# First gated embedding: input products ahead of the second gate, x of the first column half added and flipped while the second gate is multiplied

## The chip, the cores and the metric

The kernel runs on one core of a Trainium2 chip. The time is that of the device, in microseconds, for one execution of the whole program. Work is done by TensorE (matrix products), VectorE and ScalarE (elementwise), GpSimd (a little) and SyncE, which issues the loads.

## What is computed

Fourteen stages on an activation x of 256 rows by 1024 columns, in float32. The change is in the tenth, the first "gated embedding", and in what surrounds it. From the reference, cut to that stage and its neighbours:

```python
x = x + 0.5 * swiglu(rms_norm(x, ln_ffn2[i]), ffn2_w_gu[i], ffn2_w_down[i])    # stage g2.0
gate = jax.nn.sigmoid(rms_norm(x, ln_ple[i]) @ ple_w_gate[i])                  # stage pl0 (i = 0)
x = x + gate * (p[i] @ ple_w_in[i])
x = x + 0.5 * swiglu(rms_norm(x, ln_ffn1[i]), ffn1_w_gu[i], ffn1_w_down[i])    # stage g1.1 (next i)
```

The gate's weight is 1024 by 1024, `p[i]` is 256 by 256 and `ple_w_in[i]` 256 by 1024.

## The kernel before

**Split products.** A product of float32 matrices is made of three passes: each operand is split into a rounded high part and a low part (the difference), and high by high, high by low and low by high are added in PSUM (`mm3`). For a weight, ScalarE copies the high part from `ring` to `WH` (`hi`) and VectorE subtracts to give the low part in `WL` (`lo`), in parts of 1024 columns; two pieces of weights fit in `WH` and `WL`. For x, TensorE transposes it ("flip", L208) into PSUM, ScalarE scales the result by the norm's gain into the high part `XH` (`flip_act`) and VectorE forms the low part `XL` (`flip_dve`); both lie in the tile `XBt`. A flip is done in two halves: half 0 is columns 0 to 511 of x (eight blocks of 128 become kt 0 to 3), half 1 the rest (kt 4 to 7). Within a half, `i` is one of two groups of 128 rows. The norm's row factor is applied later, so products can start before the sum of squares is known; the squares are ScalarE's (`square`).

**The gated embedding `pl0`** (`ple`). The gate is computed in two column halves n = 0 and 1, each from two pieces of weights, `pl_g0_0.0`, `pl_g0_0.1` and `pl_g1_0.0`, `pl_g1_0.1`. `tms_pe` multiplies one gate: for each piece c (kt 4c to 4c+3) and each i, 12 matmuls of 512 columns. So a gate is 48 matmuls. `p @ w_in` ("input products") is not split: 8 float32 matmuls of 512 columns, read straight from `ring` and recorded as 16 passes. ScalarE takes a tanh of each gate result (two per gate), VectorE does two operations per half and i: `T2 = (tanh + 1) * product`, then `x = 0.5 * T2 + x`. The semaphore value named `pl0.x{i}{n}` says that x of rows i, columns n is there. The transposes of the next stage's flip (`follow[t].pe`) wait on it.

**The next stage `g1.1`** (`ffn`) has 22 pieces `g1.1.0` to `g1.1.21` of 3072 columns: parts 0 and 1 are gate and up weights, part 2 the output weights. Pieces 0 and 1 need 48 matmuls of 256 columns each, from piece 2 on a product takes 32 matmuls; after the product of piece j (from 2 on) follow 12 matmuls with the output weights of piece j-2 (they read `HHt` and `HLt`).

**Queues.** Each engine has one list of instructions, in the order in which the stage functions are called; no engine overtakes within its list. `ring` has three slots of 3072 columns, taken in turn. SyncE's list of loads is fixed: a piece's first part is loaded when parts 0 and 1 of the piece that held the slot have been split, its last 1024 columns (`rear`) when part 2 has been. `pl_p_0` and `pl_i_0`, the operands of the input products, take a slot each; the loads of `g1.1.1` and `g1.1.2` wait for the last input product, whose semaphore value has the name `pl_i_0`. PSUM's eight banks are given out in the order in which TensorE's list asks for them.

Of the kernel before, what the change touches and what calls it, by code (L numbers as in the profile page):

```python
# [248 lines left out]
def build(nc, wts, vecs, rows4, rowb, cons, rgw, xin, out):  # L249
    ctx = ExitStack()  # L250
    with ctx:
# [29 lines left out]
        X = v3(Xt[:, :], 2)  # L281
# [237 lines left out]

        n_ss, n_x, n_r, n_h, n_t, n_q, n_s4, n_s5, n_f = sm(2), sm(2), sm(2), sm(2), sm(2), sm(2), sm(4), sm(4), sm(2)  # L520
        DG, RB = work[:, NW - 512:NW - 256], work[:, NW - 256:NW]
        follow = {}

        def flip_pe(P, t, src, half, key):

# [28 lines left out]
        def flip_pool(G, t):  # L554

            for q in range(4):
                sl = slice(2 * q, 2 * q + 2)
                G.wait_ge(f"{t}.xl{q}")
                G.tt(XF[:, sl, :], XH[:, sl, :].bitcast(F32), XL[:, sl, :].bitcast(F32), ADD, inc=f"{t}.xf" if q == 3 else None,
                     back=2 if q else 1)  # L560

        def unscaled(t, g, prev, rows, whole=False):


            SQ4 = work[:, 2048:4096].rearrange("p (n i d) -> p n i d", n=2, i=2)

            def pe(P, half):
                flip_pe(P, t, X, half, lambda i, half: f"{prev}.x{i}{half}")

            def act(A, between=None, early=None):  # L570
                def square(half, i):
                    A.wait_ge(f"{prev}.x{i}{half}")
                    A.act(SQ4[:, half, i, :], X[:, i, half * 512:half * 512 + 512], ACT.Square,
                          accum_out=n_s4[:, 2 * half + i:2 * half + i + 1], inc=(f"{t}.sq" if half else f"{t}.sqa") if i else None)

                flip_act(A, t, g, 0)
                if early:
                    early(A)
                square(0, 0)
                square(0, 1)  # L580
                if between:
                    between(A)
                square(1, 0)
                flip_act(A, t, g, 1)
                square(1, 1)

            def dve(V, q):
                if q < 4:
                    flip_dve(V, t, g, q)
                if q in (4, 5):  # L590
                    V.wait_ge(f"{t}.sq")
                    V.tt(n_ss, n_s4[:, 0:2], n_s4[:, 2:4], ADD)
                    V.ts(n_x, n_ss, 1.0 / 1024, EPS, MUL, ADD)
                    V.rsqrt0(n_r, n_x)
                if q in (4, 6):
                    for k in range(3):
                        V.rsqrt1(n_r, n_x, n_t, inc=f"{t}.nr" if k == 2 else None)
                    for i in range(2) if rows else ():
                        V.ts(DG[:, hs(i)], IDN, n_r[:, i:i + 1], None, MUL, None, inc=f"{t}.dg" if i else None, back=1 + i)

            follow[prev] = Stage(pe, act, dve, (lambda G: flip_pool(G, t)) if whole else None)
            return follow[prev]

# [120 lines left out]
        def ffn(t, g, prev):  # L724
# [113 lines left out]
            def act(A):  # L838
                if first:
                    wh, _, w = start_cut()  # L840
                    A.wait_ge(f"{t}.0:lda")
                    A.act(wh[:, :, 0:256], w[:, :, 0:256], ACT.Copy, inc=f"{t}.0:hia")
                    norm.act(A, early=start_act)
                else:
                    hi(A, f"{t}.0", (0, 1))
                    norm.act(A)
                hi(A, f"{t}.1", (0, 1))
                for j in range(NFF):
                    nx2, b = ahead(f"{t}.{j}"), j % 2
                    if j >= NARROW:  # L850
                        A.wait_ge(f"{t}.{j}:g")
                        A.act(LW[:, b, 0:256], ps[f"{t}.g{j}"][:, 256:512], ACT.Copy, inc=f"{t}.gl{j}")
                    hi(A, nx2, (0,) if j else (0, 1))
                    A.wait_ge(f"{t}.gm{j}")
                    A.act(SG[:, b, :], GU[:, b, 0:256], ACT.Silu, inc=f"{t}.sg{j}")
                    if j < NFF - 1:
                        hi(A, f"{t}.{j}", (2,))
                    if j >= NARROW:
                        A.wait_ge(f"{t}.{j}:u")
                        A.act(LW[:, b, 256:512], ps[f"{t}.u{j}"][:, 256:512], ACT.Copy, inc=f"{t}.ul{j}")  # L860
                    if j < NFF - 1:
                        hi(A, nx2, (1,))
                    if j < NFF - 1:
                        A.wait_ge(f"{t}.h{j}")
                        if j >= 2:
                            A.wait_ge(f"{t}.{j - 2}:d")
                        A.act(HH[:, b, :], H[:, b, :], ACT.Copy, inc=f"{t}.hh{j}")
                    else:
                        split_last_act(A, 0)
                        for i in range(2):  # L870
                            A.wait_ge(f"{t}.h{j}{i}")
                            A.act(HH[:, 2, hs(i)], H[:, b, hs(i)], ACT.Copy, inc=f"{t}.hh{j}{i}")
                        split_last_act(A, 1)
                        hi(A, nx2, (1,))
                    if first:
                        params_act(A, j)
                    if t == "g1.0" and j in (6, 7):
                        A.wait_ge(f"{t}.nf")
                        A.act(X[:, j - 6, :], X[:, j - 6, :], ACT.Copy, scale=n_f[:, j - 6:j - 5], inc=f"{t}.xf{j}")

            def dve(V):
# [5 lines left out]
                        start_dve(V, u)  # L887
                else:
                    lo(V, f"{t}.0", (0, 1))
                for q in range(2 if first else 1, 4):  # L890
                    norm.dve(V, q)
                if t == "g1.0":
                    norm.dve(V, 4)
# [2216 lines left out]
        def ple(t, li, prev):  # L3110
# [3 lines left out]
            T2 = buf(512)  # L3114
            gate = lambda n: (f"pl_g{n}_{li}.0", f"pl_g{n}_{li}.1")

            def pe(P):
                for n in range(2):
                    tms_pe(P, gate(n), 4, 512, t, head=None if n else norm)
                if li:  # L3120
                    return
                wp, wi = v3(raw("pl_p_0"), 2), v3(raw("pl_i_0"), 2)
                for n in range(2):
                    for i in range(2):
                        if n and i and t in follow:
                            follow[t].pe(P, 0)
                        use = f"{t}.pi{n}{i}"
                        ps.take(use)
                        P.wait_ge("pl_p_0:ld", "pl_i_0:ld", *ps.free(use))
                        for kt in range(2):  # L3130
                            last = n == 1 and i == 1 and kt == 1
                            P.mm(ps[use], wp[:, kt, hs(i)], wi[:, kt, n * 512:n * 512 + 512], kt == 0, kt == 1,
                                 inc=("pl_i_0" if last else use) if kt else None)
                        ps.give(use, f"{t}.pie{n}{i}")

            def act(A):
                norm.act(A)
                for n in range(2):
                    hi(A, ahead(gate(n)[0]))
                    if n == 0:  # L3140
                        hi(A, ahead(gate(n)[1]))
                    for i in range(2):
                        last = gate(n)[1]
                        A.wait_ge(last if i else f"{last}:i0", f"{t}.nh")
                        A.act(TH[:, n, i, :], ps[f"{last}/{i}"], ACT.Tanh, scale=n_h[:, i:i + 1], inc=f"{last}.e{i}")

            def dve(V):
                for q in range(1, 5):
                    norm.dve(V, q)
                    if q == 1:  # L3150
                        lo(V, gate(0)[1], (0,))
                V.ts(n_h, n_r, 0.5, None, MUL, None, inc=f"{t}.nh")
                for n in range(2):
                    lo(V, ahead(gate(n)[0]))
                    if n == 0:
                        lo(V, ahead(gate(n)[1]))
                for n in range(2):
                    for i in range(2):
                        xv = X[:, i, n * 512:n * 512 + 512]
                        V.wait_ge(f"{t}.pie{n}{i}" if li else "pl_i_0" if n and i else f"{t}.pi{n}{i}", f"{gate(n)[1]}.e{i}")  # L3160
                        if li:
                            V.stt(T2, TH[:, n, i, :], 1.0, PI[:, n, i, :], ADD, MUL)
                        else:
                            V.stt(T2, TH[:, n, i, :], 1.0, ps[f"{t}.pi{n}{i}"], ADD, MUL, inc=f"{t}.pie{n}{i}")
                        V.stt(xv, T2, 0.5, xv, MUL, ADD, inc=f"{t}.x{i}{n}")
                    if n == 0 and t in follow:
                        follow[t].dve(V, 0)

            def pool(G):
                lo(G, ahead(gate(0)[0]))  # L3170
# [302 lines left out]
```

## Time and profile before

| what | value |
|---|---|
| three runs | 2108.29, 2112.36, 2113.53 us; median 2112.36 |
| the profiled execution | 2112.04 us, of which its span is 2110.2 us |
| granted TensorE clock, mean | 0.997 |
| TensorE busy | 2084.3 us, 99% |
| weight loads busy | 1790.8 us, 85% |
| VectorE busy | 1541.8 us, 73% |
| ScalarE busy | 1289.6 us, 61% |

The span runs from the first instruction to the last; the time has some 1.8 us more. All stretches named below are microseconds from the span's start. Stage `pl0` and the start of `g1.1` lie between 1575 and 1615 us. A TensorE instruction counts as busy from its start to a modelled end, and neighbours overlap, so the distance between starts says more than the duration.

### The profile page before, as it was taken

The numbers are of one execution on the slowest core, as the hardware profiler recorded it, in microseconds if no ns is written. First come the engines' busy times: TensorE is split into PE (matmuls) and PEld (weight loads), VectorE is DVE, ScalarE is ACT, GpSimd is POOL, SyncE is SP. The second block draws the span as 40 slices with busy tenths as digits, with TensorE's granted clock in tenths as the row PEclk, the third lists the DMA queues.
The fourth block names the chain that finished last, engine by engine and source line by source line (L and its number), as shares of the span: only waits on it lengthen the run. The fifth ranks groups of instructions, "written<-read, shape, count | busy, mean of one in ns | idle before, by whom it ended". The sixth has DMA issues, their size and how long they took to land.

```text
span 2110.2 us, 33620 instructions
## 1 busy us (share of the span) xinstructions
PE 2084.3 (99%) x12545; PEld 1790.8 (85%) x12545; DVE 1541.8 (73%) x2787; ACT 1289.6 (61%) x2170; POOL 61.5 (3%) x51
## 2 busy tenths in 40 slices
PE   8999999999999999999999999999999999999999
PEld 7888988888888877888888897888887888988887
DVE  6777888677766677766877677587677776868676
ACT  6656766556555367655665677565565555666555
POOL 0001000000000400000000001000000000000000
PEclk9999999999999999999999999999999999999999
DMA  7553445454555532555455351145445544445452
GB/s 271 185 209 127 159 180 189 180 192 167 210 181 166 180 121 111 193 196 190 166 194 197 126 193 61 71 174 206 180 155 196 203 181 155 164 155 187 180 195 94
DMA packets 74827, 360.76 MB, mean 171 GB/s; under 512 B 17000, under 2 KB 18024, under 8 KB 43816
## 3 DMA queue, kind: packets, MB, share of 16 engines
q1 hardware_dynamic: 74240, 358.08, 46.8%
q8 instruction: 98, 1.61, 0.3%
q14 instruction: 65, 0.53, 0.1%
q0 software_dynamic: 128, 0.26, 0.0%
q10 hardware_dynamic: 296, 0.27, 0.0%
HBM read 357.54 MB, written 1.05 MB: 170 GB/s over the span
## 4 chain that ended last, share of the span: by engine, by line
PE 89%; DVE 5%; ACT 4%; issue 1%; DMA 1%; SPq 0%; DVEq 0%; POOL 0%; ACTq 0%; POOLq 0%
PE ps L203 87%; ACT work L193 2%; DVE WL L121 2%; PE ps L208 2%; DVE work L121 1%; ACT WH L193 1%; DMA ring<-wts 1%; ACT XBt L193 1%; DVE XBt L132 1%; DVE work L132 0%; DVE small L121 0%; DVE small L132 0%; DVE Xt L132 0%; DVE work L158 0%; DVE Xt L121 0%
## 5 line engine op out<-in xcount | busy, mean ns | idle before, releaser
L203 PE MATMUL ps<-XBt,WH 128*128 128x512 f32 (+1 forms) x4144 | 1197.3, 355 | 4.4 <-DVE XBt L132 1.9
L121 DVE TENSOR_TENSOR WL<-ring,WH 128x1024 fp32r<-128x1024 f32 (+2 forms) x653 | 791.3, 1212 | 345.3 <-ACT WH L193 297.9
L193 ACT ACTIVATE WH<-ring 128x1024 fp32r<-128x1024 f32 (+1 forms) x667 | 698.8, 1048 | 345.4 <-PE ps L203 260.9
L203 PE MATMUL ps<-XBt,WL 128*128 128x256 f32 x3352 | 886.5, 280 | 0.0
L203 PEld LDWEIGHTS ps<-XBt,WH 128*128 128x128 f32 x4144 | 718.5, 190 | 105.9 <-DVE WL L121 4.5
L203 PEld LDWEIGHTS ps<-XBt,WL 128*128 128x128 f32 x3352 | 635.6, 190 | 26.6
L203 PE MATMUL ps<-WH,HHt 128*128 128x512 f32 x712 | 278.8, 392 | 0.9 <-DVE WL L121 0.7
L203 PE MATMUL ps<-WH,HLt 128*128 128x512 f32 x712 | 277.2, 389 | 0.0
L203 PE MATMUL ps<-WL,HHt 128*128 128x512 f32 x712 | 277.1, 389 | 0.0
L193 ACT ACTIVATE work<-ps 128x256 f32<-128x256 f32 (+4 forms) x444 | 179.3, 408 | 60.4 <-PE ps L203 21.8
L193 ACT ACTIVATE work<-work 128x256 f32<-128x256 f32 (+6 forms) x222 | 98.7, 445 | 171.1 <-DVE work L121 167.9
L121 DVE TENSOR_TENSOR work<-ps,work 128x256 f32<-128x256 f32 (+3 forms) x376 | 166.1, 442 | 42.4 <-ACT work L193 4.1
L203 PE MATMUL ps<-WH,XBt 128*128 128x512 f32 (+3 forms) x528 | 164.6, 382 | 1.8 <-DVE WL L121 1.3
L203 PEld LDWEIGHTS ps<-WH,HLt 128*128 128x128 f32 x712 | 133.7, 188 | 28.7
L203 PEld LDWEIGHTS ps<-WL,HHt 128*128 128x128 f32 x712 | 133.8, 188 | 28.4
L193 ACT ACTIVATE HHt<-work 128x256 fp32r<-128x256 f32 (+1 forms) x185 | 76.0, 411 | 129.1 <-DVE work L121 127.8
L203 PEld LDWEIGHTS ps<-WH,HHt 128*128 128x128 f32 x712 | 133.7, 188 | 23.4 <-DVE HLt L121 1.4
L121 DVE TENSOR_TENSOR work<-work 128x256 f32<-128x256 f32 (+2 forms) x338 | 142.1, 421 | 12.1 <-ACT work L193 0.7
L203 PE MATMUL ps<-work 64*64 64x64 f32 (+16 forms) x1256 | 116.7, 281 | 2.1 <-ACT work L193 1.9
L203 PEld LDWEIGHTS ps<-WH,XBt 128*128 128x128 f32 x528 | 97.4, 188 | 23.1 <-DVE WL L121 2.9
L203 PEld LDWEIGHTS ps<-work 64*64 64x64 f32 (+6 forms) x1256 | 88.6, 158 | 24.2 <-issue 10.4
L203 PE MATMUL ps<-WL,XBt 128*128 128x512 f32 (+3 forms) x264 | 99.0, 375 | 0.0
(137 smaller groups left out, 1076.8 us busy)
## 6 DMA issues: line engine op xcount, KB each, us to landing
ring<-wts SPq DMA_DIRECT2D x240, 1024.0 KB, 5.8
ring<-wts SPq DMA_DIRECT2D x185, 512.0 KB, 3.8
ring<-wts SPq DMA_DIRECT2D x10, 256.0 KB, 5.0
ring<-wts SPq DMA_DIRECT2D x1, 1152.0 KB, 5.0
Xt<-x SPq DMA_DIRECT2D x4, 256.0 KB, 5.7
out<-Xt SPq DMA_DIRECT2D x4, 256.0 KB, 2.0
ring<-wts SPq DMA_DIRECT2D x1, 768.0 KB, 6.5
work<-wts SPq DMA_DIRECT2D x1, 512.0 KB, 4.6
```

The lines of the kernel that those rows point to most:

```text
L121: self.done(self.e and self.e.tensor_tensor(out, a, b, op), inc)
L132: self.done(self.e and self.e.scalar_tensor_tensor(out, a, s, b, op0, op1), inc)
L193: self.done(self.e and self.e.activation(out, a, f, **kw), inc)
L203: inst = self.e and self.e.matmul(out, l, r, start=start, stop=stop)
L208: inst = self.e and self.e.transpose(out, a, ident)
```

## The change

Four things are done in another order; one call site of a function is moved, nothing is computed otherwise.

- TensorE: the input products of n = 0 (4 matmuls) stand between the two gates; those of n = 1 (4 matmuls) and the transposes of x's half 0 for `g1.1` (8) stand in the middle of the second gate, after its first piece.
- VectorE: x of columns n = 0 is added before the weights of `g1.1.0` are split; the low parts of the flip's half 0 are formed before x of n = 1 is added.
- ScalarE: the high parts of the flip's half 0 are made before the second gate's tanh.
- VectorE: part 2 of `g1.1.0` is no longer split there, but in `ffn`'s loop, at j = 0.

The second gated embedding (`li` = 1) keeps its order.

```diff
-            def act(A, between=None, early=None):
+            def act(A, between=None, early=None, flipped=False):
...
-                flip_act(A, t, g, 0)
+                if not flipped:
+                    flip_act(A, t, g, 0)
...
+            flip_ahead[prev] = lambda A: flip_act(A, t, g, 0)
...
-                    norm.act(A)
+                    norm.act(A, flipped=True) if prev == "pl0" else norm.act(A)
...
-                for q in range(2 if first else 1, 4):
+                for q in range(2 if first or prev == "pl0" else 1, 4):
...
+            def inputs_pe(P, n):
+
+                wp, wi = v3(raw("pl_p_0"), 2), v3(raw("pl_i_0"), 2)
+                for i in range(2):
+                    use = f"{t}.pi{n}{i}"
+                    ps.take(use)
+                    P.wait_ge("pl_p_0:ld", "pl_i_0:ld", *ps.free(use))
+                    for kt in range(2):
+                        last = n == 1 and i == 1 and kt == 1
+                        P.mm(ps[use], wp[:, kt, hs(i)], wi[:, kt, n * 512:n * 512 + 512], kt == 0, kt == 1,
+                             inc=("pl_i_0" if last else use) if kt else None)
+                    ps.give(use, f"{t}.pie{n}{i}")
+
+            def between_pe(P, c, i):
+
+                if c == 0 and i:
+                    inputs_pe(P, 1)
+                    follow[t].pe(P, 0)
+
             def pe(P):
-                for n in range(2):
-                    tms_pe(P, gate(n), 4, 512, t, head=None if n else norm)
-                if li:
-                    return
...
+                tms_pe(P, gate(0), 4, 512, t, head=norm)
+                if not li:
+                    inputs_pe(P, 0)
+                tms_pe(P, gate(1), 4, 512, t, between=None if li else between_pe)
 
             def act(A):
...
+                    if n and t in follow:
+                        flip_ahead[t](A)
                     for i in range(2):
                         last = gate(n)[1]
...
+            def added_dve(V, n):
+
+                for i in range(2):
+                    xv = X[:, i, n * 512:n * 512 + 512]
+                    V.wait_ge(f"{t}.pie{n}{i}" if li else "pl_i_0" if n and i else f"{t}.pi{n}{i}", f"{gate(n)[1]}.e{i}")
+                    if li:
+                        V.stt(T2, TH[:, n, i, :], 1.0, PI[:, n, i, :], ADD, MUL)
+                    else:
+                        V.stt(T2, TH[:, n, i, :], 1.0, ps[f"{t}.pi{n}{i}"], ADD, MUL, inc=f"{t}.pie{n}{i}")
+                    V.stt(xv, T2, 0.5, xv, MUL, ADD, inc=f"{t}.x{i}{n}")
...
-                for n in range(2):
-                    lo(V, ahead(gate(n)[0]))
-                    if n == 0:
-                        lo(V, ahead(gate(n)[1]))
...
+                for k in range(2):
+                    lo(V, ahead(gate(0)[k]))
+                added_dve(V, 0)
+                lo(V, ahead(gate(1)[0]), (0, 1))
+                if t in follow:
+                    for q in range(2):
+                        follow[t].dve(V, q)
+                added_dve(V, 1)
```

How the lists of instructions move is seen best on VectorE and ScalarE, the engines for which TensorE waits in this place. VectorE's list at `pl0`'s end, before; `WL<-ring,WH` splits a part of a weight, `work<-work,ps` and `Xt<-work,Xt` are the two operations that add to x, `XBt<-ps,vt,XBt` is one block of the flip's low part, and `small` belongs to the norm:

```order
L126 TENSOR_SCALAR small<-small 128x2
L121 TENSOR_TENSOR WL<-ring,WH 128x1024 x7
L132 SCALAR_TENSOR_TENSOR work<-work,ps 128x512
L132 SCALAR_TENSOR_TENSOR Xt<-work,Xt 128x512
L132 SCALAR_TENSOR_TENSOR work<-work,ps 128x512
L132 SCALAR_TENSOR_TENSOR Xt<-work,Xt 128x512
L132 SCALAR_TENSOR_TENSOR XBt<-ps,vt,XBt 128x256 x2
```

And VectorE's list at the same place now:

```order
L126 TENSOR_SCALAR small<-small 128x2
L121 TENSOR_TENSOR WL<-ring,WH 128x1024 x4
L132 SCALAR_TENSOR_TENSOR work<-work,ps 128x512
L132 SCALAR_TENSOR_TENSOR Xt<-work,Xt 128x512
L132 SCALAR_TENSOR_TENSOR work<-work,ps 128x512
L132 SCALAR_TENSOR_TENSOR Xt<-work,Xt 128x512
L121 TENSOR_TENSOR WL<-ring,WH 128x1024 x2
L132 SCALAR_TENSOR_TENSOR XBt<-ps,vt,XBt 128x256 x4
```

Of the seven splits four are ahead of the first addition (those of the second gate's weights), two (`g1.1.0`, parts 0 and 1) behind it, and the seventh (part 2) has gone to the loop of `g1.1`. The piece of the difference where it turns up again, on VectorE at j = 0 of that loop, between the product `H` of piece 0 (`work<-work,ps`) and its low part `HLt`:

```order
 L121 TENSOR_TENSOR WL<-ring,WH 128x1024
 L121 TENSOR_TENSOR work<-work,ps 128x256
+L121 TENSOR_TENSOR WL<-ring,WH 128x1024
 L121 TENSOR_TENSOR HLt<-work,HHt 128x256
 L121 TENSOR_TENSOR work<-ps,work 128x256
```

The low part `HLt` of piece 0 now stands one split later, and so does what waits for it. ScalarE's list from the copies of `g1.1.0`'s high parts to the squares of `g1.1`'s norm, as the difference shows it (`work<-ps,small` is a tanh, `XBt<-ps,vt` one block of the flip's high part, `work,small<-Xt` a square with its sum):

```order
 L193 ACTIVATE work<-ps,small 128x512 x2
 L193 ACTIVATE WH<-ring 128x1024 x3
+L193 ACTIVATE XBt<-ps,vt 128x256 x4
 L193 ACTIVATE work<-ps,small 128x512 x2
-L193 ACTIVATE XBt<-ps,vt 128x256 x4
 L193 ACTIVATE work,small<-Xt 128x512 x3
 L193 ACTIVATE XBt<-ps,vt 128x256 x4
```

The flip's half 0 has gone ahead of the second gate's tanh; the three squares and the flip's half 1 stay behind it, in the same order.

## Rows read from the trace of the kernel before

**Rows 1.** The profile page: span, and busy time by engine

```profile
span 2110.2 us, 33620 instructions
...
PE 2084.3 (99%) x12545; PEld 1790.8 (85%) x12545; DVE 1541.8 (73%) x2787; ACT 1289.6 (61%) x2170; POOL 61.5 (3%) x51
```

**Rows 2.** Waits of TensorE, 1586 to 1790 us: waiting group, releaser, us, times, longest

```profile
PE ps L208 <- DVE Xt L132: 1.0, 2, 0.9
```

**Rows 3.** Busy time by stage: stretch, us, each engine (instructions), clock, DMA share, GB/s

```profile
1586.81:1597.69 10.88, 10.88 (x49) 9.01 (x48) 3.47 (x3) 4.48 (x5) 0.00 (x0) 1.00 0.65 242
1597.69:1605.61 7.92, 7.73 (x26) 3.69 (x24) 6.03 (x9) 4.03 (x8) 0.00 (x0) 1.00 0.00 0
1605.61:1614.28 8.67, 7.67 (x58) 6.77 (x57) 7.36 (x15) 6.65 (x15) 0.00 (x0) 1.00 0.84 317
```

**Rows 4.** TensorE in order of time: start us, busy us, instruction, [idle before, releaser]

```profile
1597.69 5.31 PE L203 MATMUL ps<-ring 128*128 128x512 f32 x12
...
1603.63 0.66 PE L208 MATMUL ps<-ct,Xt 128*128 128x128 f32 x4 [0.19 <-DVE Xt L132]
...
1607.43 0.66 PE L208 MATMUL ps<-ct,Xt 128*128 128x128 f32 x4
1608.95 0.66 PE L208 MATMUL ps<-ct,Xt 128*128 128x128 f32 x4 [0.86 <-DVE Xt L132]
1609.55 0.50 PE L203 MATMUL ps<-XBt,WH 128*128 128x256 f32 x2
...
1614.28 0.51 PE L203 MATMUL ps<-XBt,WH 128*128 128x256 f32 x2
...
1626.16 0.39 PE L203 MATMUL ps<-WH,HHt 128*128 128x512 f32 x1
```

**Rows 5.** The same: the first matmul of piece 4's product

```profile
1637.20 0.39 PE L203 MATMUL ps<-XBt,WH 128*128 128x512 f32 x1
```

**Rows 6.** ScalarE in order of time

```profile
1588.17 1.41 ACT L193 ACTIVATE work<-ps,small 128x512 f32<-128x512 f32 x2
1595.56 3.37 ACT L193 ACTIVATE WH<-ring 128x1024 fp32r<-128x1024 f32 x3 [5.98 <-DMA ring<-wts]
...
1605.77 0.63 ACT L193 ACTIVATE work<-Xt 128x512 f32<-128x512 f32 x1
...
1607.41 0.63 ACT L193 ACTIVATE work<-Xt 128x512 f32<-128x512 f32 x1
...
1609.43 1.57 ACT L193 ACTIVATE XBt<-ps,vt 128x256 fp32r<-128x256 f32 x4 [1.29 <-PE ps L208]
...
1628.10 1.06 ACT L193 ACTIVATE WH<-ring 128x1024 fp32r<-128x1024 f32 x1
```

**Rows 7.** VectorE in order of time

```profile
1586.80 2.55 DVE L121 TENSOR_TENSOR WL<-ring,WH 128x1024 fp32r<-128x1024 f32 x2 [0.15 <-ACT WH L193]
1596.66 3.88 DVE L121 TENSOR_TENSOR WL<-ring,WH 128x1024 fp32r<-128x1024 f32 x3 [7.31 <-ACT WH L193]
...
1601.37 0.69 DVE L132 SCALAR_TENSOR_TENSOR Xt<-work,Xt 128x512 f32<-128x512 f32 x1
...
1610.30 1.86 DVE L132 SCALAR_TENSOR_TENSOR XBt<-ps,vt,XBt 128x256 fp32r<-128x256 f32 x4 [0.41 <-ACT XBt L193]
...
1613.00 2.55 DVE L121 TENSOR_TENSOR WL<-ring,WH 128x1024 fp32r<-128x1024 f32 x2 [0.17 <-ACT WH L193]
...
1621.58 0.42 DVE L121 TENSOR_TENSOR work<-work,ps 128x256 f32<-128x256 f32 x1
1622.48 0.42 DVE L121 TENSOR_TENSOR HLt<-work,HHt 128x256 fp32r<-128x256 f32 x1 [0.48 <-ACT HHt L193]
```

**Rows 8.** SyncE's loads into `ring` issued in 1600 to 1610: issue, then landing times

```profile
L196 SPq DMA_DIRECT2D ring<-wts x6: 327/461/686, 1606.0 to 1608.7; - x6
...
DMA to landing us min/median/max: 5.2/8.7/12.2
```

**Rows 9.** The same for the two issued in 1626 to 1627

```profile
DMA to landing us min/median/max: 3.8/4.8/5.9
```

More of the change, by code:

```diff
@@ L521, in build @@
         DG, RB = work[:, NW - 512:NW - 256], work[:, NW - 256:NW]
-        follow = {}
+        follow, flip_ahead = {}, {}
         def flip_pe(P, t, src, half, key):
@@ L3115, in ple @@
             gate = lambda n: (f"pl_g{n}_{li}.0", f"pl_g{n}_{li}.1")
-            def pe(P):
-                for n in range(2):
-                    tms_pe(P, gate(n), 4, 512, t, head=None if n else norm)
-                if li:
-                    return
-                wp, wi = v3(raw("pl_p_0"), 2), v3(raw("pl_i_0"), 2)
-                for n in range(2):
[L3124 to L3134, printed above, removed]
+            def inputs_pe(P, n):
[13 more added lines that the diff above has]
+                    follow[t].pe(P, 0)
+            def pe(P):
+                tms_pe(P, gate(0), 4, 512, t, head=norm)
+                if not li:
+                    inputs_pe(P, 0)
+                tms_pe(P, gate(1), 4, 512, t, between=None if li else between_pe)
             def act(A):
@@ L3152, in dve @@
                 V.ts(n_h, n_r, 0.5, None, MUL, None, inc=f"{t}.nh")
-                for n in range(2):
-                    lo(V, ahead(gate(n)[0]))
-                    if n == 0:
-                        lo(V, ahead(gate(n)[1]))
[L3157 to L3167, printed above, removed]
+                for k in range(2):
[6 more added lines that the diff above has]
+                added_dve(V, 1)
             def pool(G):
```

## The prediction, made before the change was run

> **What bounds the kernel now.** I read the page first. TensorE is busy for 2084.3 of 2110.2 us, the other engines for 73% at most [rows 1]. So the kernel ends when TensorE has issued its list, and a change that removes no TensorE work can only win or lose where TensorE stands still. The second view is TensorE's waits from the start of the second gate to 1790 us: the only group is the transposes waiting for x, 1.0 us in 2 waits [rows 2]. That is the whole visible prize. The third is the table by stage [rows 3]: the second gate runs from 1586.81 to 1597.69 without a gap; the input products and the first transposes take 7.92 us, of which TensorE is busy 7.73; from there to the first matmul of piece 1 it is 8.67 us with 7.67 busy. The fourth is TensorE in order of time [rows 4]: the reader is to see the transposes at 1603.63 and at 1608.95, behind idle 0.19 and 0.86 us that an addition to x ends, and the start of piece 1 at 1614.28. As rows 2 have no further wait up to 1790, everything behind 1614.28 follows that start rigidly. The question is therefore: when does TensorE start piece 1 after the change?
>
> **The change on TensorE.** The list holds the same matmuls. Gate 2, input products and transposes of half 0 last 10.88 + 7.73 = 18.61 us of work [rows 3] in either order, if none of them waits. Starting from 1586.81, the block ends at 1605.42 and not at 1605.61: 0.19 won. Does anything in it wait now?
> - Input products of n = 0: their operands were loaded long ago, and their banks held half 0 of `pl0`'s own flip, which was done before the first gate ended. Nothing.
> - A pass of an input product takes 5.31 / 12 = 0.44 us [rows 4], so the first four products (8 passes) last 3.5 us, until 1590.3. Half of the second gate is 5.4 us, until 1595.7; four more products end at 1599.2, where the transposes of half 0 ask for x.
> - x of n = 0: VectorE has split the second gate's weights by 1586.80 + 2.55 = 1589.35 [rows 7], the tanh pair ends at 1588.17 + 1.41 = 1589.6 [rows 6], the last input product at 1590.3. From then two operations of 0.7 us [rows 7] give x at about 1592. TensorE asks 7 us later. Nothing.
> - The flip's half 0 may overwrite kt 0 to 3 only when the second gate has read them, and this holds: its first piece is exactly those.
> - ScalarE's copies of `g1.1.0` end at 1595.56 + 3.37 = 1598.9 [rows 6], before the transposes are done (about 1600). It flips for 1.6 us, until 1601.7, before the tanh of i = 0 can start (about 1602.7). VectorE splits `g1.1.0` from 1596.66 for two parts, 2.6 of the 3.88 us [rows 7], then four low parts in 1.86 us, until about 1603. They are needed at 1605.42. Nothing.
>
> New borders between float32 and split matmuls: there are two more than before. The trace has no row that prices one alone; below, nothing, as they may be seamless; above, 0.2 us each, the idle that stands before the transposes at 1603.63 [rows 4]. I take 0 and keep up to 0.4 us for the range.
>
> **Behind the second gate.** Before, TensorE had the last input product as cover while VectorE added x. Now the gate itself ends there, and this is what is late next:
> - The last gate matmul starts 0.23 us (10.88 / 48) before 1605.42 and takes 0.39 (as the one at 1626.16 [rows 4]); the tanh of i = 1 starts at about 1605.61. Two tanh take 1.41 us [rows 6], so one has a pitch of about 0.77.
> - VectorE: tanh done at 1606.25, two operations, x at 1607.7. TensorE meanwhile does the first 12 matmuls of piece 0 and four transposes. Before, the second took place 1.82 us after the start of the first (1605.61 to 1607.43), so it now reaches the last transposes at 1605.42 + 1.82 + 0.4 = 1607.64. It waits 0.1 us in place of 0.86. The bank of `tr3` comes free only with the last `T2`, at about 1607.0, which hides in the same wait.
> - ScalarE: behind the tanh (1606.38) stand three squares, pitch (1607.41 - 1605.77) / 2 = 0.82 us [rows 6], 2.46 us in all. The flip of half 1 starts at **1608.84**; before, it started at 1609.43 [rows 6]. From this flip the old order runs unchanged: flip, fourth square, copy of `g1.1.1`'s high part, split (at 1613.00, waiting for ScalarE [rows 7]), piece 1 at 1614.28. That is 1614.28 - 1609.43 = 4.85 us. New start of piece 1: 1608.84 + 4.85 = **1613.69**, 0.59 us earlier.
> - TensorE's own order gives less: the last transposes at 1607.75, matmuls from 0.6 us later (1608.95 to 1609.55 [rows 4]), 12 of them until 1609.9, a wait of 0.3 us for the first low part of half 1 (0.87 us behind the flip's start, plus 0.47 [rows 6, 7], 1610.2), then 24 matmuls at 0.12 us, until 1613.25. So ScalarE's chain decides by 0.4 us.
>
> In other words: of 1.05 us of known waits, 0.86 shrinks to 0.1 and 0.19 goes, but TensorE then stands before the low part of half 1 and before piece 1, since the three squares are now behind a tanh that starts when the gate ends.
>
> **What moves farther on.** (a) Loads of `g1.1.1` and `g1.1.2` wait for the last input product, which is 6.4 us earlier (1599.2 for 1605.6). The burst that began at 1606.0 [rows 8] begins at about 1599.6; ScalarE wants piece 1 at 1611.3, so this is cover it already had. (b) Part 2 of `g1.1.0` is split at j = 0, after `H`: 1621.58 + 0.42 + 0.1 - 0.59 = 1621.5, until 1622.7. `HLt` of piece 0 ends at about 1623.3, and TensorE reads it at 1626.16 - 0.59 = 1625.6 [rows 4, 7]. Slack 2.3 us, cost nothing. (c) SyncE's list: the rear load of `g1.1.3` waits for that split, and the front load of `g1.1.4` is queued behind it. They now leave at about 1622.8 and 1623.2. The like pair issued at 1626.6 landed after 3.8 and 5.9 us [rows 9]; so `g1.1.4` lands at 1629.1. ScalarE wants it at 1628.10 - 0.59 = 1627.5 [rows 6] and will wait 1.6 us, a new wait. Copy 1.06 and split 1.28 us later it is ready at 1631.5; TensorE starts piece 4 at 1637.20 - 0.59 = 1636.6 [rows 5]. Slack 5.1 us, cost nothing. From j = 1 on part 2 is split early in the round, as before.
>
> **Sum.** -0.59 us against the profiled execution's own 2112.04 (2110.2 of span and 1.8 around it): 2111.45. The median of the runs shown is 0.32 above that execution, so I put the time at 2112.36 - 0.6 = 2111.8. The three runs lie 5.2 us apart, nine times the effect. A measurement of this kernel can tell 0.3%, 6.3 us, from no change.
>
> **A rule weighed against rows.** The load share of the input products' stage is 3.69 of 7.92 us, that of the second gate 9.01 of 10.88 [rows 3]. The Trainium skill (Perfetto Trace Analysis, Identifying the Most-Contended Engine) says that matmul busy time is no good measure of distance to the limit and that the share of weight loads is; by it the input products' stage has some 4.2 us of air (7.92 - 3.69, an estimate), and moving them among the gate's matmuls could let it out. By the rows a pass takes 0.44 us wherever its load ends, so my sum has nothing for it.
>
> **Rivals.**
> - *Passes run closer in the new place* (the air in that stage is real): 16 passes at the gate's 0.23 instead of 0.44 us would give 3.4 us more, 2108.4. Against it: within the row of twelve no pass comes closer, and the new rows have the same neighbours within a product.
> - *The gain is not given back*: ScalarE's chain is shorter than I add it up and no wait is left between 1605.42 and piece 1. Then piece 1 starts at 1605.42 + 7.67 = 1613.09, 1.2 us earlier, 2111.2.
> - *Borders cost*: at 0.2 us or more each, plus a late tanh, piece 1 starts where it did; 2112.4.
> - *SyncE's queue (slower)*: `g1.1.4` lands late. The longest landing in these rows is 12.2 us [rows 8]: 1623.2 + 12.2 + 2.3 = 1637.7, TensorE waits 1.1 us at piece 4, net 0.5 slower, 2112.9. It decides from a landing of 11.1 us on. For it: an issue blocked at the head of the only load queue. Against it: the long landings belong to a burst of six issues within 2.7 us; here there are two, and their like took 5.9.
>
> **How the numbers follow.** Forecast (0.2 to 1.2 us earlier, with the second rival as its end) 0.74; borders eat it 0.10; SyncE's queue 0.08; closer passes 0.04; something that I don't see 0.04. All named cases lie between 2108.4 and 2112.9, within 0.3% of before; only the last reaches beyond it, and I add as much again for medians that differ by themselves: faster 0.03, same 0.94, slower 0.03. The range must hold the spread of the medians more than the mechanism: mechanism -3.9 to +0.5 us around 2112.4, and the runs' own 2108.3 to 2113.5. I take 2107 to 2116.
>
> **What would show it.** In the changed trace: no gap on TensorE from the gate's start to the end of the block, so piece 0 starts 18.6 us after the second gate; the last transposes of half 1 idle for 0.1 to 0.3 us; ScalarE's flip of half 1 begins right after a square and waits for nothing; piece 1 starts 26.9 us after the second gate began (27.5 before), released by a split; ScalarE waits for a load 1 to 2 us at its copy of `g1.1.4`; TensorE has no wait from there on. Wrong would be a wait of TensorE at piece 4, a gap in the middle of the gate, a lower granted clock in this stretch, or a shift of times elsewhere in the kernel.

## The result: slower by 0.36%, and the profile after

The changed kernel takes 2119.49 us (median of 5 runs, 2117.69 to 2120.01), the kernel before 2109.68 (5 runs beside it, 2108.12 to 2113.53). The ratio is 1.0036, 95% interval 1.0026 to 1.0047: 7.6 us more, 5.5 to 9.9 (the two medians by themselves lie 9.8 apart). I had forecast 2111.8 us and no change that can be measured.

TensorE's waits in the changed kernel between 1586 and 1810 us (waiting group, releaser, us, times, longest); before, this stretch held one group of 1.0 us [rows 2]:

```profile
PE ps L203 <- DMA ring<-wts: 4.6, 1, 4.6
PE ps L208 <- DVE Xt L132: 0.3, 1, 0.3
PE ps L203 <- DVE WL L121: 0.3, 1, 0.3
```

A wait on a load is new, and it is one single wait. TensorE in order of time shows the place:

```profile
1578.65 1.03 PE L208 MATMUL ps<-ct,Xt 128*128 128x128 f32 x8
...
1587.47 0.39 PE L203 MATMUL ps<-WH,XBt 128*128 128x512 f32 x1
1592.50 5.83 PE L203 MATMUL ps<-ring 128*128 128x512 f32 x8 [4.64 <-DMA ring<-wts]
1597.77 0.79 PE L203 MATMUL ps<-WH,XBt 128*128 128x512 f32 x1
1598.40 0.39 PE L203 MATMUL ps<-WL,XBt 128*128 128x512 f32 x1
...
1603.64 3.59 PE L203 MATMUL ps<-ring 128*128 128x512 f32 x8
1607.07 1.04 PE L208 MATMUL ps<-ct,Xt 128*128 128x128 f32 x8
...
1614.86 0.73 PE L208 MATMUL ps<-ct,Xt 128*128 128x128 f32 x4
1615.88 0.66 PE L208 MATMUL ps<-ct,Xt 128*128 128x128 f32 x4 [0.29 <-DVE Xt L132]
...
1621.50 0.50 PE L203 MATMUL ps<-XBt,WH 128*128 128x256 f32 x2 [0.27 <-DVE WL L121]
```

The first gate ends at 1587.69 (its last matmul starts at 1587.47 and the next would follow 0.22 us later). Then TensorE does nothing until 1592.50: the first input product waits for its operand. It is seen too that the eight passes at 1592.50 take 5.27 us to the next instruction, while the eight at 1603.64 take 3.43. (What follows differs, a gate matmul there and transposes here; an undisturbed row of eight passes ahead of a gate matmul takes 3.03 us, as the run with the early load shows below.) The table of this kernel by stage (stretch, us, busy time of TensorE, weight loads, VectorE, ScalarE, GpSimd, then granted clock, share of the DMA engines, GB/s) says why:

```profile
1587.69:1592.50 4.81, 0.17 (x1) 0.03 (x1) 2.44 (x2) 2.43 (x3) 0.00 (x0) 0.74 0.82 273
1592.50:1597.77 5.27, 5.27 (x8) 2.22 (x9) 1.38 (x2) 0.00 (x0) 0.00 (x0) 0.59 0.61 252
1597.77:1607.07 9.30, 9.30 (x34) 6.14 (x33) 3.83 (x4) 3.17 (x3) 0.00 (x0) 1.00 0.00 0
```

The granted clock falls while TensorE idles and is 0.59 on the mean over the passes behind the gap, so most of them run at the lower level, 1.2 GHz: with a granted clock of either 1 or 0.5, a mean of 0.59 is about four fifths of the stretch at the lower one (an estimate). Behind 1597.77 it is 1.00 again.

One measure serves for all runs below, since it does not contain what varies elsewhere: the distance from the end of the first gate to the first matmul of piece 1. The end of the first gate is 9.04 us behind the start of its own eight transposes (before, 1586.81 and 1577.77; here 1578.65 and 1587.69). Before it is 1614.28 - 1586.81 = **27.47 us** [rows 3, 4], now 1621.50 - 1587.69 = **33.81 us**, 6.3 more. Predicted were 26.9.

The load that is waited for, as SyncE issued it, in the changed kernel (the one load into `ring` in the window 1580 to 1590 us; first and last start, then issue to landing):

```profile
L196 SPq DMA_DIRECT2D ring<-wts x1: 328/328/328, 1587.6 to 1587.6; - x1
...
DMA to landing us min/median/max: 4.8/4.8/4.8
```

And the same load in the kernel before, which stands in none of the rows that I had picked:

```profile
L196 SPq DMA_DIRECT2D ring<-wts x1: 328/328/328, 1586.7 to 1586.7; - x1
...
DMA to landing us min/median/max: 6.3/6.3/6.3
```

This is `pl_i_0`, 1 MB. It takes the slot of `pl_g1_0.0` in `ring`, which is free when VectorE has split part 1 of that piece. Before, that was at 1586.7, just as the first gate ended, and the load landed at 1593.0. The first input product came at 1597.69 [rows 4], 4.7 us later: the second gate was its cover. The change asks for it at the end of the first gate.

### The profile page after: what moved, and what is told of

Its sections match the earlier page's. It is cut to its first block, busy times and chain, and to the rows that moved or that the text cites. A ratio compares the mean times of both kernels' runs of the same rounds, so it can differ in the third digit from the quotient of the medians.

```text
span 2117.3 us, 33620 instructions
## 1 busy us (share of the span) xinstructions
PE 2085.5 (98%) x12545; PEld 1790.2 (85%) x12545; DVE 1542.2 (73%) x2787; ACT 1289.5 (61%) x2170; POOL 59.5 (3%) x51
## 4 chain that ended last, share of the span: by engine, by line
PE 89%; DVE 4%; ACT 4%; issue 1%; DMA 1%; SPq 0%; ACTq 0%; DVEq 0%; POOL 0%; POOLq 0%
PE ps L203 88%; ACT work L193 2%; PE ps L208 2%; DVE WL L121 1%; ACT WH L193 1%; DMA ring<-wts 1%; ACT XBt L193 1%; DVE work L121 1%; DVE XBt L132 0%; DVE small L132 0%; DVE small L121 0%; DVE work L132 0%; DVE work L158 0%; DVE Xt L121 0%; ACT L193 0%
```

## Experiments

Theory A: the loss is the wait for `pl_i_0`, plus the lower clock that the gap brings. Theory B: it comes from the new order on VectorE and ScalarE, from the split of part 2 or from SyncE's queue. Each version ran 5 to 12 times, the kernel before 5 times beside the change and 27 or 29 times beside the others.

| run | median us | ratio to before, 95% interval | end of the first gate to piece 1, us |
|---|---|---|---|
| before | 2109.7 to 2111.4 (by set of runs) | 1 | 27.47 |
| the change | 2119.49 | 1.0036 (1.0026 to 1.0047) | 33.81 |
| only n = 0 ahead | 2119.79 | 1.0044 (1.0031 to 1.0056) | 34.38 |
| n = 0 in the middle | 2111.04 | 1.0001 (0.9992 to 1.0011) | 27.11 |
| early load | 2110.82 | 0.9998 (0.9989 to 1.0006) | 26.77 |
| wait filled | 2115.4 | 1.0022 (1.0014 to 1.0031) | 31.71 |
| early load, squares ahead | 2110.7 | 0.9999 (0.9991 to 1.0008) | 26.48 |
| early load, old order | 2112.0 | 1.0006 (0.9997 to 1.0015) | 27.07 |
| middle, squares ahead | 2111.89 | 1.0003 (0.9995 to 1.0012) | 27.48 |

The last column comes from one profiled execution each, so its small differences have no spread of their own beside them.

### One part alone: the products of n = 0 ahead of the second gate

The edit against the kernel before:

```diff
             def pe(P):
-                for n in range(2):
-                    tms_pe(P, gate(n), 4, 512, t, head=None if n else norm)
...
+                tms_pe(P, gate(0), 4, 512, t, head=norm)
+                if not li:
+                    inputs_pe(P, 0)
+                tms_pe(P, gate(1), 4, 512, t)
+                if not li:
+                    inputs_pe(P, 1)
```

(`inputs_pe` as in the change; `follow[t].pe` stays between the two products of n = 1.)

> The order of before, with only the four input products of n = 0 moved ahead of the second gate; transposes, VectorE's and ScalarE's lists as before. Theory A (the products ahead of the second gate wait for the load of their weight pl_i_0, 4.8 us, and the clock falls meanwhile, 2.2 us more): the whole loss is here, TensorE idles 4 to 5 us before the first pass of an input product, the granted clock there is under 1, piece 1 starts 34 to 35 us after the end of the first gate (27.5 before, 33.8 in the change), and the time is 6 to 8 us over before. Theory B (the loss comes from the new order on VectorE and ScalarE, the split part of piece 0 or SyncE's queue): 27 to 28 us and the time of before.

TensorE in order of time in this kernel:

```profile
1581.45 1.03 PE L208 MATMUL ps<-ct,Xt 128*128 128x128 f32 x8
...
1590.27 0.39 PE L203 MATMUL ps<-WH,XBt 128*128 128x512 f32 x1
1595.46 5.91 PE L203 MATMUL ps<-ring 128*128 128x512 f32 x8 [4.80 <-DMA ring<-wts]
1600.81 0.79 PE L203 MATMUL ps<-WH,XBt 128*128 128x512 f32 x1
1601.44 0.39 PE L203 MATMUL ps<-WL,XBt 128*128 128x512 f32 x1
...
1624.87 0.50 PE L203 MATMUL ps<-XBt,WH 128*128 128x256 f32 x2
```

The same gap and the same slow passes, with nothing else of the change in the kernel. The distance is 1624.87 - (1581.45 + 9.04) = 34.38 us, so the moved products alone cost 6.9, and the rest of the change, which came on top in the changed kernel, gave 0.6 back. The time is 9.3 us over before (6.5 to 11.8); I had expected 6 to 8, which that interval overlaps.

### That part undone: the same products in the middle of the second gate

The edit against the changed kernel:

```diff
                 if c == 0 and i:
+                    inputs_pe(P, 0)
                     inputs_pe(P, 1)
+                if c == 1 and not i:
                     follow[t].pe(P, 0)
...
-                if not li:
-                    inputs_pe(P, 0)
```

> The change, but the four input products of n = 0 stand in the middle of the second gate, ahead of those of n = 1, and the transposes of half 0 after the first row group of its second piece; all else as in the change. Theory A: by then (5.4 us later) the load is there, TensorE idles under 1 us, clock 1.00, piece 1 starts 27 to 28 us after the end of the first gate, the time is within 1 us of before. Theory B: everything that it blames is still in the kernel, so the loss of 6 to 7 us stays.

```profile
1575.17 1.03 PE L208 MATMUL ps<-ct,Xt 128*128 128x128 f32 x8
...
1589.66 7.03 PE L203 MATMUL ps<-ring 128*128 128x512 f32 x16
...
1605.27 0.44 PE L208 MATMUL ps<-ct,Xt 128*128 128x128 f32 x2 [0.38 <-DVE work L132]
1606.00 0.66 PE L208 MATMUL ps<-ct,Xt 128*128 128x128 f32 x4 [0.28 <-DVE Xt L132]
1611.32 0.51 PE L203 MATMUL ps<-XBt,WH 128*128 128x256 f32 x2 [0.27 <-DVE WL L121]
```

The load of `pl_i_0` in this kernel:

```profile
L196 SPq DMA_DIRECT2D ring<-wts x1: 328/328/328, 1584.1 to 1584.1; - x1
...
DMA to landing us min/median/max: 4.9/4.9/4.9
```

It lands at 1589.0, and the sixteen passes start at 1589.66, 5.4 us behind the end of the first gate, with no wait before them. The distance is 27.11 us, and the time is that of before. Theory B's suspects are all still in this kernel, the transposes inside the gate, the lists of VectorE and ScalarE, the late split, SyncE's queue. They cost nothing that can be measured, so Theory B falls. The wait of 0.38 us on `work` is the bank of the last transposes, which the last `T2` frees; I had it as hidden, and with the products placed later it is not.

### The change with its operand there

In the changed kernel, `pl_p_0` and `pl_i_0` go into free columns of `work` while g2.0 runs:

```diff
-        OWN = ("fin_g", "nsa_gt", "nsa_w2", "pl_p_1")
+        OWN = ("fin_g", "nsa_gt", "nsa_w2", "pl_p_1", "pl_p_0", "pl_i_0")
...
         def raw(name):
+            if name == "pl_p_0":
+                return work[:, 8192:8704]
+            if name == "pl_i_0":
+                return work[:, 8704:10752]
...
+                if name == "g2.0.8":
+                    S.wait_ge("g2.0.2:d")
+                    for own_name, wide_cols in (("pl_p_0", 512), ("pl_i_0", 2048)):
+                        a = begin[own_name]
+                        S.dma(raw(own_name), wts[a:a + 128 * wide_cols].rearrange("(p n) -> p n", p=128), f"own_{own_name}", inc=f"{own_name}:ld")
```

> The change in its own order, but pl_p_0 and pl_i_0 are loaded during stage g2.0 into 2560 free columns of the tile work and take no slot of ring. Theory A: no wait before the input products, clock 1.00; what I forecast for the change comes true here: piece 1 starts 26.9 us after the end of the first gate (0.6 less than before), the time is 0 to 1 us under before. Theory B: the loss of 6 to 7 us stays.

TensorE, then ScalarE, in order of time:

```profile
1583.40 3.59 PE L203 MATMUL ps<-work 128*128 128x512 f32 x8
1586.43 0.80 PE L203 MATMUL ps<-WH,XBt 128*128 128x512 f32 x1
1587.07 0.39 PE L203 MATMUL ps<-WL,XBt 128*128 128x512 f32 x1
```

```profile
1602.30 0.69 ACT L193 ACTIVATE work<-ps,small 128x512 f32<-128x512 f32 x1 [2.03 <-PE ps L203]
1603.09 0.63 ACT L193 ACTIVATE work<-Xt 128x512 f32<-128x512 f32 x1
...
1605.35 1.55 ACT L193 ACTIVATE XBt<-ps,vt 128x256 fp32r<-128x256 f32 x4
```

The eight passes and the gate's first matmul take 1587.07 - 1583.40 = 3.67 us, eight steps of 0.43 and one of 0.23, as such passes and matmuls take elsewhere: the borders between float32 and split products cost nothing. Piece 1 starts at 1610.17, 26.77 us after the end of the first gate (the transposes start at 1574.36); I had predicted 26.88 for the change. So every term of that sum held except the one for the operands. The early load itself doesn't make this agreement: from the first gate matmul behind the passes to piece 1 it is 1610.17 - 1586.43 = 23.74 us here and 1621.50 - 1597.77 = 23.73 in the changed kernel. The time is that of before.

### The clock by itself

In the changed kernel TensorE gets 20 matmuls to do while it waits for the load. Their results are overwritten, so they only keep it at work:

```diff
                     ps.take(use)
+                    if n == 0 and i == 0:
+                        P.wait_ge(*ps.free(use))
+                        for _ in range(20):
+                            P.mm(ps[use], XH[:, 4, hs(0)], XB[:, 4, :], True, True)
                     P.wait_ge("pl_p_0:ld", "pl_i_0:ld", *ps.free(use))
```

> The change, with 20 matmuls of 512 columns (4.5 us) whose results are overwritten, put ahead of the first input product, where TensorE waits for the load; they use a bank and blocks of x that nobody changes meanwhile. If the clock's fall is a cost of its own on top of the wait (Theory A), it stays at 1.00, the eight passes take 3.4 us and not 5.3, and piece 1 starts about 31.6 us after the end of the first gate, 2.2 less than the change's 33.8; the time is some 2 us under the change's. If the passes were slow for another reason (their operands just loaded, the transition from split matmuls), they are slow here too and 33.8 stays.

By stage, and in order of time:

```profile
1585.34:1590.19 4.85, 4.70 (x21) 3.59 (x20) 2.43 (x2) 2.44 (x3) 0.00 (x0) 1.00 0.79 270
1590.19:1593.30 3.11, 3.11 (x8) 1.44 (x9) 1.08 (x2) 0.00 (x0) 0.00 (x0) 1.00 0.99 412
```

```profile
1593.30 0.80 PE L203 MATMUL ps<-WH,XBt 128*128 128x512 f32 x1
1593.94 0.40 PE L203 MATMUL ps<-WL,XBt 128*128 128x512 f32 x1
```

The wait for the load is as long (4.85 us), but TensorE works through it and the clock is 1.00. From the first pass to the gate's second matmul it is 1593.94 - 1590.19 = 3.75 us; in the change it was 1598.40 - 1592.50 = 5.90. The distance is 31.71 us, 2.1 less than in the change. So the 6.3 us divide into 4.8 of waiting and 2.2 of a lower clock behind it, less the 0.6 to 0.7 that the new order gives. The times of the two kernels differ less clearly than the traces: the ratios to before are 1.0036 and 1.0022, some 3 us apart, and their intervals overlap.

### Is there a version that wins?

The flip of half 1 starts late since three squares lie between it and the last tanh. Two of them need only x of n = 0 and can be taken sooner. The edit goes on top of the early load and is cut here to the new place; at the old place the two squares go:

```diff
                     for i in range(2):
+                        if n and t in follow:
+                            square_ahead[t](A, i)
                         last = gate(n)[1]
```

> The early load with the change's order, and the two squares of x of columns 0 to 511 taken on ScalarE ahead of the second gate's two tanh, one before each, instead of behind them. Theory A with my reading of the end of the block (three squares behind the last tanh hold up the flip of half 1): the flip starts 0.6 us sooner, at the transposes' end, no square directly ahead of it but one; piece 1 starts some 26.0 to 26.3 us after the end of the first gate (26.8 in the early load, 27.5 before), time 1 to 1.5 us under before, hardly to be told from it by times. If the squares were not what ScalarE's chain hangs on, 26.8 stays.

ScalarE now:

```profile
1608.28 0.69 ACT L193 ACTIVATE work<-ps,small 128x512 f32<-128x512 f32 x1 [1.21 <-PE ps L203]
1609.06 0.63 ACT L193 ACTIVATE work<-Xt 128x512 f32<-128x512 f32 x1
...
1611.00 1.57 ACT L193 ACTIVATE XBt<-ps,vt 128x256 fp32r<-128x256 f32 x4 [1.22 <-PE ps L208]
```

The flip waits for the transposes (1.22 us) and no longer for a square. It starts 2.72 us behind the last tanh, 3.05 in the early load (1605.35 - 1602.30): only 0.33 sooner, not 0.6, as the transposes' end takes over. Piece 1 starts after 26.48 us, where I had expected 26.0 to 26.3.

A control: the order of before, with the early load.

> Control: the order of before with the early load of pl_p_0 and pl_i_0. If the early load by itself gives or takes time (ring has its slots free sooner, a load of 1.3 MB lies in g2.0 instead), it shows here. I expect nothing: piece 1 starts 27.5 us after the end of the first gate, the time is that of before within 1 us, so that the early load's gain of 0.7 us in the change's order is that of the order.

The distance is 27.07 us (transposes at 1580.95, piece 1 at 1617.06), so the early load gives 0.4 of its own, against my expectation. Its trace has the eight transposes of half 0 in one row, without the 0.19 us of idle of before [rows 4]. `pl_p_0` and `pl_i_0` no longer take slots of `ring`, so the weights of `g1.1.0` come sooner: ScalarE starts to copy them 4.3 us behind the end of the first gate (1594.33), 8.8 us before, and VectorE is through with them when x can be added. The order's own share of the early load's gain is then 27.07 - 26.77 = 0.3 us.

```profile
1606.03 1.04 PE L208 MATMUL ps<-ct,Xt 128*128 128x128 f32 x8
...
1611.73 0.66 PE L208 MATMUL ps<-ct,Xt 128*128 128x128 f32 x4 [0.86 <-DVE Xt L132]
```

Last, the two squares ahead without the early load, in the kernel with all input products in the middle of the second gate.

> No early load: all input products in the middle of the second gate, and the two squares ahead of the tanh as in the run with the early load. In the run without the squares ahead, piece 1 started 27.1 us after the end of the first gate. Here x of n = 0 is there later and VectorE's flips delay the last additions, so the squares help less: 26.4 to 27.0 us expected, time 0 to 1 us under before.

This missed: 27.48 us, 0.4 worse than the middle place without the squares ahead. ScalarE has no air there. The tanh of i = 0 comes behind the flip and a square, VectorE's addition with it, and a new wait stands before the last transposes:

```profile
1606.52 0.44 PE L208 MATMUL ps<-ct,Xt 128*128 128x128 f32 x2 [0.33 <-DVE Xt L132]
1607.39 0.44 PE L208 MATMUL ps<-ct,Xt 128*128 128x128 f32 x2 [0.42 <-DVE work L132]
1608.11 0.66 PE L208 MATMUL ps<-ct,Xt 128*128 128x128 f32 x4 [0.29 <-DVE Xt L132]
```

No version is faster than before in its times; the best by the trace, early load with squares ahead, starts piece 1 1.0 us sooner, which its 11 runs can't tell from nothing (0.9991 to 1.0008).

## Why the prediction was wrong

**The step that failed** is the first bullet of "The change on TensorE": "Input products of n = 0: their operands were loaded long ago". No row stood behind it. My rows of issues and landings were all of loads behind 1600 us, and two others spoke against it: the DMA engines are 65% busy during the second gate, with 242 GB/s over 10.88 us, or 2.6 MB [rows 3], and ScalarE gets the next load in SyncE's list, `g1.1.0`, only at 1595.56 [rows 6]. The slot of `pl_i_0` follows from the list of loads and the three slots (that of `pl_g1_0.0`), its release (the split at 1586.80 [rows 7] belongs to the piece after it, so the split that frees the slot ended just before) could be read, and the longer of a like pair of loads took 5.9 us [rows 9]. From these alone: issue at about 1586.7, landing at 1592.6, and a new wait of almost 6 us for an instruction moved to 1586.8. The term was nothing; it measured 4.8 us. The miss is larger than the times 2111.8 and 2119.49 show: I had set out from a median of 2112.36 where five runs gave 2109.68, and the effect was 7.6 us slower in place of 0.6 faster.

**The clock** was in no term and no rival, only in the list of what would prove me wrong. It is a cost of the gap and not of the change's order: 2.2 us, shown by the run with the wait filled.

**What held.** The block without waits, the late additions and ScalarE's chain: 26.88 us predicted, 26.77 measured once the operand was there, and the same 23.7 us behind the slow passes in the changed kernel. In the changed kernel too, behind the slow passes: the last transposes idle 0.29 us (0.1 to 0.3 was said), the flip of half 1 starts directly behind a square, and piece 1 waits for a split. The late load in SyncE's list is there too and costs nothing, as said. ScalarE waits for it 1.16 us at its copy of `g1.1.4`, where 1.6 were predicted:

```profile
1636.96 1.06 ACT L193 ACTIVATE WH<-ring 128x1024 fp32r<-128x1024 f32 x1 [1.16 <-DMA ring<-wts]
```

Behind the start of piece 1 TensorE has one wait to the end of the program, 0.2 us in the changed kernel and 0.3 before, both behind 1810 us. VectorE's late split of part 2 had its slack.

**The rivals.** Closer passes did not come: the distance between passes is 0.43 us in every place at clock 1.00. The share of weight loads, by which I had opened that rival, pointed to no gain here. The borders cost nothing. None of the five cases was the real one; the 0.04 for something unseen is where it lay, and for such a case I had given slower by over 0.3% a chance of 0.03. Its measured ratio, 1.0036, is only just beyond that bound. Two sums in the prediction are slightly off and decide nothing: 24 matmuls at 0.12 us from 1610.2 end at 1613.1 and not at 1613.25, and 2108.4 lies 4.0 us under 2112.4, not 3.9.

**What stays open.** The times of the change and of the one-part run are 7.6 and 9.3 us over before, the stage accounts for 6.3 and 6.9; the intervals hold both (5.5 to 9.9 and 6.5 to 11.8). For the change the two profiled executions say where the rest lies. Their spans are 7.1 us apart: 6.3 in the stage, 0.9 ahead of the end of the first gate (1587.69 and 1586.81), which the change doesn't touch and which lies anywhere from 1584.2 to 1590.5 in the kernels without the early load, and -0.1 behind the start of piece 1. Outside the span the time has 2.1 to 2.2 us in all runs of the six kernels that have the change's new order on VectorE and ScalarE, and about 1.8 before, in the one-part run and in the old order with the early load. These some 0.35 us come with the change too; their cause is not known. The one-part run has nothing of them; its profiled execution, the slowest of its five, has 3.7 us more ahead of the end of the first gate.

## What to carry to other kernels

Where an instruction is moved ahead, list each thing that it reads and find for each the row that says when it landed in the trace of before, its own load too; "loaded long ago" is a number, the landing's time against the new place. In a ring of slots a load starts when an older piece is let go, so an operand used late is loaded late, and the work that stood ahead of its use was its cover. Here a wait of 4.8 us on TensorE cost 2.2 us more than its length, since the work behind it ran at the lower clock; the waits of 0.19 and 0.86 us before lie in stretches with a granted clock of 1.00 [rows 3, 4].

## What I had not expected of the hardware

- A gap of 4.8 us on TensorE, in a kernel whose mean granted clock is 0.996, is followed by a granted clock of 0.59 over 5.27 us, and eight passes and one matmul take 5.90 us in place of 3.67. In the gap itself the granted clock is 0.74 on the mean.
- Eight float32 passes right behind split matmuls, and split matmuls right behind them, cost no more than in a row of their own: 3.67 us for eight passes and one matmul.
- `pl_i_0`, 1 MB, landed 4.8 to 5.0 us after its issue in the changed kernel, in the one-part run, in both with the products in the middle and in the one with the wait filled, and 6.3 us in the kernel before. The loads behind it don't explain that: in before as in the change the next one left 2.7 us later (1586.7 and 1589.4, 1587.6 and 1590.3). Why it took longer there is not known.
